# Attention steps regrouped in the mixing stages: outputs and scores in one step, transposes alone, two empty steps

## What is computed

```python
mix = token_mixing(x, w_in[l], conv_a_w[l], diff_lambda[l], ...)      # three branches
x = layer_norm(ALPHA * x + mix, ...)
x = layer_norm(ALPHA * x + conv_ffn(x, ...), ...)
```

```python
merged = gates[0] * (y_a @ w_branch[0]) + gates[1] * (y_b @ w_branch[1]) + gates[2] * (y_c @ w_branch[2])
return merged @ w_o
```

## Time and profile before

| | |
|---|---|
| time, median of 3 runs | 3725.37 us (3721.77 to 3727.17) |
| the profiled execution | 3719.88 us, its span 3718.0 us |
| TensorE matmul busy | 3569.8 us, 96% |
| VectorE busy | 2054.9 us, 55% |
| ScalarE busy | 1423.8 us, 38% |
| chain that ended last, share of TensorE | 80% |
| granted TensorE clock, mean of the span | 0.984 |

### The profile page before, as it was taken

The page is one execution under the profiler, slowest core; times in us unless marked ns, Lnnn a source line. Parts: engine busy times, 40 slices in busy tenths (PEclk is TensorE's granted clock), DMA queues, the critical chain, the costliest instruction groups (busy, mean ns, idle before and its releaser), DMA issues.

```text
span 3718.0 us, 49044 instructions
## 1 busy us (share of the span) xinstructions
PE 3569.8 (96%) x19338; PEld 2854.9 (77%) x19338; DVE 2054.9 (55%) x3664; ACT 1423.8 (38%) x2210; POOL 154.3 (4%) x270
## 2 busy tenths in 40 slices
PE   8999999999999999999999888999999899889999
PEld 6777677887777767777777857788888799667887
DVE  4756666777766666677885545523232531753333
ACT  3456633442325565243323344321212332742222
POOL 0000000000001000000001200100000230000000
PEclk9999999999999999999998999999999899999999
DMA  4122233334431222434353100112121111212322
GB/s 169 71 80 69 83 133 113 136 125 173 141 119 64 69 76 89 159 106 154 128 204 109 57 1 12 51 47 84 39 82 44 66 67 57 69 46 74 112 92 85
DMA packets 65942, 339.95 MB, mean 91 GB/s; under 512 B 6832, under 2 KB 8368, under 8 KB 39984
## 3 DMA queue, kind: packets, MB, share of 16 engines
q1 hardware_dynamic: 65712, 336.82, 26.0%
HBM read 328.40 MB, written 8.39 MB: 91 GB/s over the span
## 4 chain that ended last, share of the span: by engine, by line
PE 80%; DVE 13%; ACT 5%; issue 1%; DMA 1%; POOL 0%; DVEq 0%; ACTq 0%; SPq 0%; POOLq 0%
PE ps L1857 23%; PE ps L1859 22%; PE ps L1858 22%; PE ps L1846 4%; DVE wl L2125 3%; PE ps L1993 3%; PE ps L1866 2%; DVE junk L2170 1%; DVE ha L2133 1%; ACT wh L2012 1%; DVE tt L2133 1%; DVE hl L2133 1%; DVE u L2125 1%; PE ps L1873 1%; ACT opb L2113 1%
## 5 line engine op out<-in xcount | busy, mean ns | idle before, releaser
L2125 DVE TENSOR_TENSOR wl<-raw,wh 128x2048 fp32r<-128x2048 f32 (+2 forms) x275 | 545.5, 1984 | 401.6 <-ACT wh L2012 383.9
L2012 ACT ACTIVATE wh<-raw 128x2048 fp32r<-128x2048 f32 (+2 forms) x275 | 457.3, 1663 | 756.0 <-PE ps L1859 752.4
L1857 PE MATMUL ps<-hh,wh 128*128 128x512 f32 (+1 forms) x1184 | 427.9, 361 | 13.7 <-DVE hl L2133 9.0
L1858 PE MATMUL ps<-hl,wh 128*128 128x512 f32 (+1 forms) x1184 | 421.7, 356 | 0.0
L1859 PE MATMUL ps<-hh,wl 128*128 128x512 f32 (+1 forms) x1184 | 421.6, 356 | 0.0
L1857 PE MATMUL ps<-xhb,wh 128*128 128x512 f32 x848 | 369.9, 436 | 13.5 <-DVE xlb L2125 12.8
L1859 PE MATMUL ps<-xhb,wl 128*128 128x512 f32 x848 | 336.4, 397 | 0.0
L1858 PE MATMUL ps<-xlb,wh 128*128 128x512 f32 x848 | 336.2, 396 | 0.0
L1857 PE MATMUL ps<-xha,wh 128*128 128x512 f32 x704 | 281.0, 399 | 8.0 <-DVE wl L2125 4.0
L1858 PE MATMUL ps<-xla,wh 128*128 128x512 f32 x704 | 279.2, 397 | 0.0
L1859 PE MATMUL ps<-xha,wl 128*128 128x512 f32 x704 | 279.1, 396 | 0.0
(11 more groups left out here) (308 smaller groups left out, 6845.9 us busy)
## 6 DMA issues: line engine op xcount, KB each, us to landing
raw<-in_wts SPq DMA_DIRECT2D x199, 1024.0 KB, 4.8
lt<-in_wts SPq DMA_DIRECT2D x110, 512.0 KB, 3.4
raw<-in_wts SPq DMA_DIRECT2D x44, 512.0 KB, 3.4
raw<-in_wts SPq DMA_DIRECT2D x28, 448.0 KB, 3.2
x_scratch<-xt SPq DMA_DIRECT2D x3, 2048.0 KB, 11.1
xt<-x_scratch SPq DMA_DIRECT2D x3, 2048.0 KB, 7.8
oe<-in_relb SPq DMA_DIRECT2D x16, 384.0 KB, 3.6
bt<-in_big SPq DMA_DIRECT2D x1, 2688.0 KB, 9.2
```

The source lines that it names most:

```text
L1857: T.matmul(u.out, u.sh, u.mh, start=u.first, stop=False)
L1858: T.matmul(u.out, u.sh, u.ml, start=False, stop=False)
L2012: A.activation(u.h, u.raw, ACT.Copy).then_inc(*act.inc())
L2125: V.tensor_tensor(o_, a, b, op).then_inc(*dve.inc())
```

## The change

The order of the stages within one time t of `pipeline`, and the two rates. Now one time t takes four steps: outputs of item t-4, scores of item t and weights of item t-1 in one; the turns of item t-3; nothing; nothing. The rates go from 5.6 to 7.5 and from 6 to 8 steps in 12 ticks, so that one time t takes 6.4 ticks for branch b (36/5.6 = 6.43 before) and 6 for branch c (36/6 = 6 before).

```diff
-                    for stages in (((0, 0), (1, 1)), ((3, 4),), ((2, 3),)):
+                    for stages in (((3, 4), (0, 0), (1, 1)), ((2, 3),), (), ()):
                         for stage, lag in stages:
                             if 0 <= t - lag < n:
                                 items[t - lag][stage]()
                         yield
...
-            hook["gen"], hook["rate"] = diff_part(), 5.6
+            hook["gen"], hook["rate"] = diff_part(), 7.5
...
-                        hook["gen"], hook["rate"] = nsa_part(), 6
+                        hook["gen"], hook["rate"] = nsa_part(), 8
```

## The result

The changed kernel takes 3769.32 us (median of 4 runs, 3766.52 to 3769.7), the kernel before 3725.55 us in the same comparison; the ratio is 1.0122, 95% interval 1.011 to 1.0134. It is 44 us slower; 3767 had been forecast. The spans of the profiled executions are 3718.0 and 3764.6 us, 46.6 us apart.

What follows compares the result with a forecast made beforehand. TensorE, full in branch c, was taken as the bound. Passages -12.0, waits +21.2 and +28.2, branch b +4.1 gave +41.5 us: 3761 against the profiled execution, 3767 as a median; range 3724 to 3797 us.

Steps and rivals of the forecast that it cites:

- The bound: Branch c attention, both layers: TensorE is full, so its list sets the time; other engines count only where it waits.
- Joint passages: Outputs directly before scores save one tile-shape passage back and one in, 0.19 us at 2 x 32 places: -12 us.
- Waits from the copy's place in ScalarE's list: Branch c, layer 0: outputs wait for their turns' copy, now right behind two Exp on ScalarE: +21.2 us.
- The panel ends: Layer 0: Sigmoid with table load and `wh` precede the turns' copy; seven waits, two weaker ones in conv, 11.5 us.
- The late Exp: Layer 0: the Exp before the copy wait for VectorE, so outputs wait at six times, 9.7 us in sum.
- Layer 1, +7.0 more for its phase: Branch c, layer 1: scores one tick earlier against panels, ten waits longer by up to 0.70 us; 28.2 us in all.
- The clock, 0: Branch c: TensorE read at full granted clock in the earlier trace; no term for a fall.
- Branch b, +4.1: Branch b: outputs wait for copies behind late Exp, 1.1 us in layer 0 and 3.0 in layer 1.
- The sum: Whole kernel: passages -12.0, waits 21.2 and 28.2 in layers 0 and 1, branch b 4.1, together +41.5 us.
- The first (passages decide): Rival: copies are in time, so only the 12 us saving remains; 3708 to 3715 us, chance 0.11.
- The second (waits absorbed twice): Rival: VectorE and ScalarE catch up over several times t, only each cluster's first wait stays; +14, 3739 us, chance 0.20.
- The third (nothing absorbed): Rival: late `wh` or `wl` move with TensorE's delay, each wait stands alone; +67, 3792 us, chance 0.14 with above.

Runs made afterwards that it cites:

- the two kernels nearest to each other: Changed kernel with turns one item earlier in the last step, 3713.71 us; new rates and steps with early turns but outputs alone behind scores, 3728.48 us.
- its repeat: The changed kernel measured again, nothing changed, against the kernel before: 3772.0 us, ratio 1.0131.

## Why the prediction was right, and where it was not

*The bound.* Right: what TensorE waited in branch c is in the time, in the account above. Of the signs named, TensorE is 17 and 19 us short of the stretch (20 or more had been named), and the outputs idle for 36.5 us (45).

*Joint passages, -12 us.* The mechanism is right and the unit is right (0.20 us from output to score). The sum holds as well, as far as it can be seen: 4.2 + 6.0 = 10 us between the two kernels nearest to each other, and about 12 when the 1.6 us of waits for `wl` in one of them are allowed for. In branch b nothing had been counted; no run separates it there.

*Waits from the copy's place in ScalarE's list, +21.2 in layer 0.* Right as a mechanism, shown by the three kernels without it or with less of it (outputs one item later, turns one item earlier, no Sigmoid). In size 17.7 us. The panel ends were met well: 11.5 forecast, 12.4 measured. The late Exp were forecast with 9.7 and measured with 5.3. The step that failed there is the end of the second Exp, taken from the trace of before with one wait taken off: of the six times, the first two (2.65 and 2.1) were 1.75 and 1.15 us, the third (0.6) was 1.8, and of the last three (1.6, 0.5 and 2.2) only 0.6 us in all was left. That VectorE and ScalarE recover more during a chain of waits than the forecast let them would fit the last three; it was not tested by itself.

*Layer 1, +7.0 more for its phase.* Wrong. The idle is 18.8 us against 17.7, and with the phase of layer 0 it is 17.2: the phase is worth 1.6 us of waits. The 2.4 us by which the stretch shrank lie within what the clock moves it. "A wait longer by up to 0.70 us at ten of them" held at two places (1.15 against 1.83 us, 1.78 against 2.32), both late Exp; at the panel ends the waits are the same within 0.07 us in both phases. The forecast had ScalarE's work there fixed to the panel and the outputs one tick earlier; why that gives no longer wait was not tried.

*The clock, 0.* Missing. At about half of the places where an output waits for 1.5 us or more, 3.4 us at half clock follow, or twice that. That cost about 5.6 us in layer 0 and 9.5 us in layer 1, by the account above. The forecast took the clock as given because it was 1.00 in the earlier trace rows; but a change that makes TensorE idle for the first time in a full stretch can't read the clock from the stretch without idle.

*Branch b, +4.1.* Measured 5.5 us, and in part for another reason: outputs wait for 1.9 and 2.1 us there, but the kernel without outputs in front of scores loses the same 3 us a layer. In the changed kernel one wait for a copy to `mg`, which the forecast left out, went from 1.08 to 1.94 us in layer 0, and behind that wait 3.4 us at half clock stand in each layer's branch b. In its repeat layer 1 has the same waits without that piece and is at +1.8 instead of +2.7. How the rest of the 5.5 us is made up is open.

*The sum.* For branch c: forecast +15.2 and +22.2 (with 6.0 of the passages in each layer), measured +17.3 and +22.3. The total of +41.5 against 46.6 between the traces comes from errors that offset each other: 3.5 and 9.4 us too much wait, 15 us of clock left out in branch c, and 3 us too little for branch b and everything else. Put the measured waits into the forecast's own sum, and it gives -12.0 + 17.7 + 18.8 + 4.1 = 28.6 us, not 41.5. The direction and the main mechanism are shown; the nearness of the number is in part luck.

*The rivals.* The first (passages decide) turned out to be the behaviour of the two kernels whose copies are in time, at 3717 and 3714 us. Its mark for the change, an Exp that is early everywhere, was not met. The second (waits absorbed twice) fits only the late Exp of the branch part, where next to nothing was left. The third (nothing absorbed) fits nowhere.

## What to carry to other kernels

A consumer moved forward in the bound engine's list must be checked against the place of its producer in that engine's own list: here the copy's place, behind two Exp that wait for VectorE, or behind a table load and a weight split at a panel's end, decided it, and about 2 us at every fourth item outweighed 0.19 us at each. The remedy is not to give the joint insertion up but to give the producer one more item of distance. And where insertions are given out by a counter, the phase of the counter is a parameter to be tried on its own: it was worth 9 us in a stage that nobody had touched.

## What the runs showed of the hardware

In branch c of the changed kernel, after an idle of 1.5 to 2.6 us in a TensorE stream that was otherwise full, the granted clock fell to 0.50 (1.2 GHz) for 3.4 us, and sometimes twice that, but not after each such idle: in layer 0 after 4 of 8, in layer 1 after 5 of 9 and in the repeat after 6 of 9. The waits repeat from run to run within 0.03 us, and the clock's pieces don't (20.5 and 27 us in layer 1). Each microsecond at half clock cost about 0.44 us of the stretch. The kernel before isn't free of it either: in layer 1's branch b it has an idle of 1.75 us, without a fall of the clock; the same kernel with one tick more in the second block, which is the same list up to there, has that idle, 3.4 us at half clock behind it, and a stretch longer by 1.4 us. Where six transposes filled most of an idle, the pieces behind it became fewer by half.

The passage from a 128x64 to a 64x128 matmul took 0.20 us in all 56 places of branch c, the same as from a 128x64 matmul back to the full tile.
